# Chunked delta rule with raw keys and the inverse applied inside the scan, and another placing of the fill matmuls

## The reference

```python
g = jnp.cumsum(g.reshape(bsz, nh, n, CHUNK), axis=-1)
decay = jnp.exp(jnp.where(incl, g[..., :, None] - g[..., None, :], -jnp.inf))
kb = k * beta
a_mat = jnp.where(strict, jnp.einsum('bhncd,bhnsd->bhncs', kb, k) * decay, 0.0)
rhs = jnp.concatenate([v * beta, kb * jnp.exp(g)[..., None]], axis=-1)
sol = lax.linalg.triangular_solve(eye + a_mat, rhs, left_side=True, lower=True, unit_diagonal=True)
u_c, w_c = sol[..., :dv], sol[..., dv:]
...
def step(state, inp):
    v_new = u_i - jnp.einsum('bhcd,bhdv->bhcv', w_i, state)
    o_i = (jnp.einsum('bhcd,bhdv->bhcv', q_i, state)
           + jnp.einsum('bhcs,bhsv->bhcv', qk_i, v_new))
    state = state * jnp.exp(gl_i)[..., None, None] + jnp.einsum('bhcd,bhcv->bhdv', k_i, v_new)
    return state, o_i
...
o = _rms_norm(o_f + jnp.flip(o_b, 2), dn_gain)
```

## Time and profile before

| what | us |
|---|---|
| median of three runs | 3041.14 |
| lowest and highest | 3039.02, 3042.1 |
| span of the profiled execution | 3042.0 |
| own time of the profiled execution | not given apart from the span |
| PE busy in the span | 2950.7 |
| DVE, ACT, POOL busy | 2110.4, 1411.3, 488.3 |

### The profile page before, as it was taken

How to read it: one execution, slowest core, us unless ns; L and a number is a source line. 1 busy time by engine, 2 the same in 40 slices (tenths; PEclk the granted TensorE clock), 3 DMA queues, 4 the chain that set the end, 5 groups by cost and what they waited for, 6 DMA issues and landing times.

```text
span 3042.0 us, 51632 instructions
## 1 busy us (share of the span) xinstructions
PE 2950.7 (97%) x18980; PEld 2547.3 (84%) x18980; DVE 2110.4 (69%) x3097; ACT 1411.3 (46%) x2279; POOL 488.3 (16%) x392
## 2 busy tenths in 40 slices
PE   7999999999999999999999999999999999999998
PEld 4888888887789988777789988799988777799886
DVE  5566665446489954888789944799646986899635
ACT  3655565444356622334456622566423334566422
POOL 0213123157420011000200012100110000300012
PEclk9999999999999999999999999999999999999999
DMA  6121120213322322222323232232222222233322
GB/s 254 44 61 43 28 69 16 68 63 105 110 83 98 104 97 89 94 87 83 104 90 106 97 104 97 87 108 99 99 95 92 89 84 83 97 111 102 106 94 79
DMA packets 97248, 275.15 MB, mean 90 GB/s; under 512 B 35712, under 2 KB 36864, under 8 KB 95760
## 3 DMA queue, kind: packets, MB, share of 16 engines
q1 hardware_dynamic: 94016, 267.89, 26.5%
q10 hardware_dynamic: 2768, 4.25, 0.4%
q0 software_dynamic: 320, 1.05, 0.1%
HBM read 267.88 MB, written 5.28 MB: 90 GB/s over the span
## 4 chain that ended last, share of the span: by engine, by line
PE 87%; DVE 6%; ACT 4%; issue 2%; DMA 1%; SPq 0%; ACTq 0%; DVEq 0%
PE bank L149 16%; PE bank L151 16%; PE bank L150 16%; PE bank L2024 8%; PE bank L2025 8%; PE bank L2026 8%; PE bank L1598 1%; ACT weights_hi L137 1%; PE bank L1612 1%; PE bank L1664 1%; PE bank L2515 1%; DVE weights_lo L142 1%; PE bank L1667 1%; PE bank L1677 1%; DMA mod_weights<-w_mod 1%
## 5 line engine op out<-in xcount | busy, mean ns | idle before, releaser
L142 DVE TENSOR_TENSOR weights_lo<-weights_raw,weights_hi 128x1024 fp32r<-128x1024 f32 (+2 forms) x258 | 395.5, 1533 | 326.3 <-ACT weights_hi L137 323.0
L137 ACT ACTIVATE weights_hi<-weights_raw 128x1024 fp32r<-128x1024 f32 (+2 forms) x250 | 285.1, 1140 | 460.2 <-PE bank L151 447.8
L149 PE MATMUL bank<-x_hi,weights_hi 128*128 128x512 f32 x832 | 337.0, 405 | 5.1 <-DVE x_lo L1914 3.0
L151 PE MATMUL bank<-x_hi,weights_lo 128*128 128x512 f32 x832 | 326.4, 392 | 0.0
L150 PE MATMUL bank<-x_lo,weights_hi 128*128 128x512 f32 x832 | 325.3, 391 | 0.0
L2024 PE MATMUL bank<-sum_hi,block_hi 128*128 128x256 f32 x960 | 271.1, 282 | 4.6 <-ACT bank L2176 3.6
L150 PE MATMUL bank<-hidden_lo,weights_hi 128*128 128x512 f32 x704 | 273.9, 389 | 0.0
L149 PE MATMUL bank<-hidden_hi,weights_hi 128*128 128x512 f32 x704 | 273.9, 389 | 0.0
L151 PE MATMUL bank<-hidden_hi,weights_lo 128*128 128x512 f32 x704 | 273.9, 389 | 0.0
L2025 PE MATMUL bank<-sum_lo,block_hi 128*128 128x256 f32 x960 | 270.6, 282 | 0.0
L2026 PE MATMUL bank<-sum_hi,block_lo 128*128 128x256 f32 x960 | 269.4, 281 | 0.0
(11 more groups left out here) (451 smaller groups left out, 7466.4 us busy)
## 6 DMA issues: line engine op xcount, KB each, us to landing
raw_pair<-w_ff1in SPq DMA_DIRECT2D x42, 1024.0 KB, 4.9
raw_pair<-w_ff2in SPq DMA_DIRECT2D x42, 1024.0 KB, 4.9
weights_raw<-w_mix SPq DMA_DIRECT2D x72, 512.0 KB, 3.2
weights_raw<-w_ff1out SPq DMA_DIRECT2D x32, 704.0 KB, 4.0
weights_raw<-w_ff2out SPq DMA_DIRECT2D x32, 704.0 KB, 4.0
weights_raw<-w_tail SPq DMA_DIRECT2D x42, 512.0 KB, 3.3
mod_weights<-w_mod SPq DMA_DIRECT2D x6, 2048.0 KB, 16.4
weights_raw<-w_dn SPq DMA_DIRECT2D x24, 512.0 KB, 3.4
```

Source lines behind the costliest of these rows:

```text
L137: nc.scalar.activation(K.wh[:, slot, 0:cols], K.raw[:, slot, 0:cols], ACT.Copy).then_inc(S.wh_ready, 1)
L142: nc.vector.tensor_tensor(K.wl[:, slot, 0:cols], K.raw[:, slot, 0:cols], K.wh[:, slot, 0:cols].bitcast(F32), ALU.subtract).then_inc(S.raw_ ...
L149: nc.tensor.matmul(out, K.wh[:, slot, a:b], xh, start=start, stop=False)
L151: return nc.tensor.matmul(out, K.wl[:, slot, a:b], xh, start=False, stop=stop)
```

## The change

- The keys and queries stay raw (only silu), in `K.heads_kq`, double-buffered by group. The inverse squared key norm `K.n2` is multiplied in where systems and scores are formed, and into the decayed keys; the query norm is left to the head's final norm (`K.fq`). The transposes back and those of the decayed queries go.
- The solution is not formed. Each scan step multiplies the raw keys by the state (`against`), DVE forms the residual, PE multiplies it by the inverse (`renew`), ACT copies the new values out (`renewed`), and `grow` follows.
- Turning and systems are one loop. Tile t+1 is turned, its exponents written and its products made after the fill units of tile t. Keys and queries of all tiles go through bank 3, the exponents of all tiles through bank 4.
- Fill units: 4 more ahead of the first group, 2 per tile in the merged loop (1 in the last group), 5 in the end of the levels and up to 11 in the scan, from a budget of 12 (16 in the last two groups). The last group's scan takes the tail's slabs 8 and 9 (`AHEAD`).
- DVE's `conv` instructions are all done before the scan. The three calls of `act_head` and `act_center` inside the levels are at steps 2, 8 and 12 (two before, at 9 and 16).
- In the tail the sum of squares moves to DVE, the norm is applied by ACT on four tiles, and PE transposes the head's output instead of spreading the norm.

```diff
     def act_group(act, G):
+            if n > 0:
+                act.wait_ge(S.hss_ready, n)
+            nc.scalar.activation(K.junk[:, 0:w, :], pb[3][:, 0:128 * w].rearrange("p (c v) -> p c v", v=128), ACT.Square)\
                 .then_inc(S.hsq_ready, 1)
+            nc.scalar.activation(K.ks[:, t, 0:2, :], pb[3][:, 0:256].rearrange("p (c v) -> p c v", v=128), ACT.Copy)\
+                .then_inc(S.kt_ready, 1)
             act.wait_ge(S.tv_ready, n + 1)
+            nc.scalar.activation(K.vs[:, t, :, :], pb[7][:, 0:256].rearrange("p (j v) -> p j v", v=128), ACT.Copy)\
                 .then_inc(S.vs_ready, 1)
...
+        squares(0)
...
         for t in range(TILES):
-            if t < 4:
-                queries_back(t)
+            if t + 1 < TILES:
+                squares(t + 1)
             decays(t)
-            if t == 3 and not more:
-                act_gate(act, 1)
+            if t == 3 and more:
+                act_raw(act, G + 1, 1)
...
+        for n, (f, b, x) in enumerate(scan_steps()):
+            if n == 0:
+                continue
+            renewed(n, 0)
+            renewed(n, 1)
+            if x is not None:
+                state_out(x, (f, b))
+            if more and n in (2, 4):
+                act_head(act, G + 1, 3 + n // 2)
```

```diff
     def pe_group(pe, G, fills):
+        fill, later = fills[G], islice(fills[G + 1], 12 if G + 2 < GROUPS else 16)
         if G == 0:
             take(fill, 8)
             pe_sum_rows(pe)
+            take(fill, 4)
...
+        def turn_heads(t):
             n = TILES * G + t
+            if t > 0:
+                pe.wait_ge(S.kt_ready, n)
+            for c in range(4 if t < 4 else 2):
+                src = keys(G, c) if c < 2 else queries(G, c - 2)
+                last = nc.tensor.transpose(pb[3][:, 128 * c:128 * c + 128], src[:, lo:lo + 128], K.ident[:, :])
             last.then_inc(S.tk_ready, 1)
...
+        def rows(t):
             n = TILES * G + t
             if t > 0:
+                pe.wait_ge(S.dec_ready, n)
...
+        turn_heads(0)
+        rows(0)
+        products(0)
         for t in range(TILES):
-            if t < 4:
-                turn_queries(t)
-            rows(t)
-            products(t)
-            take(fill, 1)
+            take(fill, 2 if G < 3 else 1)
+            if t + 1 < TILES:
+                turn_heads(t + 1)
+                rows(t + 1)
+                products(t + 1)
         take(fill, 99)
...
+            if i > STEPS_INNER:
+                take(later, 1)
         correction(STEPS_LEVEL - 1)
...
         for n, (f, b, x) in enumerate(scan_steps()):
+            if n == 0:
                 continue
+            tiles = (f, b)
+            for d, t in enumerate(tiles):
+                against(n, d, t)
+            if x is not None:
+                answer(n, x, tiles)
+            take(later, 1)
+            if n == 1:
+                pe.wait_ge(S.e_ready, STEPS_LEVEL * (G + 1) + CREDIT)
+            for d, t in enumerate(tiles):
+                renew(n, d, t)
+            take(later, 2)
             if n < 5:
+                for d, t in enumerate(tiles):
+                    grow(n, d, t)
+            if x is not None:
+                if x == 0:
+                    pe.wait_ge(S.qkd_ready, 4 * G + 4)
+                inner(n, x, tiles)
+        pe.wait_ge(S.oa_ready, 4 * G + 4)
         pe.wait_ge(S.ot_ready, 8 * G + 8)
```

```diff
     def dve_group(dve, G):
         if more:
-            split_lo(dve, s + 1, 1, 1024)
-            take(conv, 8)
+            take(conv, 4)
...
             ins.then_inc(S.e_ready, 1)
-            take(conv, 1 if i < STEPS_INNER + 2 else 2)
+            take(conv, 1 if i < STEPS_FIRST else 2)
...
         state_start()
     def pe_tail(pe):
             elif kind in "up":
-                pe_slab(pe, a, b, slot, False)
+                if i not in AHEAD:
+                    pe_slab(pe, a, b, slot, False)
...
             if i in NORMED:
                 n = NORMED[i]
-                pe.wait_ge(S.nrstd_ready, n + 3)
+                pe.wait_ge(S.hsc_ready, n + 1)
                 if n > 0:
-                    pe.wait_ge(S.on_ready, n)
+                    pe.wait_ge(S.zs_used, gates_until(n - 1))
                 for t in range(4):
+                    last = nc.tensor.transpose(pb[5][:, 128 * t:128 * t + 128], K.ot[:, n, t, :], K.ident[:, :])
                 last.then_inc(S.head_wide, 1)
```

More of the change, by code:

```diff
@@ L2 @@
 from contextlib import ExitStack
-from itertools import chain
+from itertools import chain, islice
 import numpy as np
@@ L511, in make_first_memory @@
     K.dd = put("inverse_turned", [128, 3, 4, 128])
+    K.otmp = [put(f"state_out{i}", [128, 4, 128], F32, w0 + 6144 + 2048 * i) for i in range(2)]
+    K.rr = put("residual", [128, 4, 128], F32, w0 + 10240)
     K.pp = put("product", [128, 2, 256])
@@ L1148, in dve_group, with norms @@
         s = DN_SLAB + 6 * G + 8
-        def squares(t):
+        def norms(t):
             n = TILES * G + t
@@ L1234, in dve_group @@
             split_lo(dve, s + 4, 0, 1024)
+            take(conv, 6)
         else:
@@ L1670, in grow @@
-        def grow(n, tiles):
+                pe.wait_ge(S.vm_ready, G + 1)
+                pe.wait_ge(S.e_ready, STEPS_LEVEL * G + STEPS_INNER + d + 1 + CREDIT)
+            for j in range(2):
+                c = 2 * d + j
+                last = nc.tensor.matmul(pb[scan_bank(n, d)][:, part(j)], K.e[:, c, t, :], K.rr[:, c, :] if n else K.vs[:, t, j, :],
+                                        start=True, stop=True)
+            last.then_inc(S.uw_made, 1)
+        def grow(n, d, t):
+            pe.wait_ge(S.vn_ready, 12 * G + 2 * n + d + 1)
+            for j in range(2):
+                c = 2 * d + j
+                last = nc.tensor.matmul(pb[scan_bank(n, d)][:, part(j)], K.ks[:, t, c, :], K.vn[:, c, :], start=True, stop=True)
+            last.then_inc(S.su_ready, 1)
@@ new lines, in against, with answer @@
+        def against(n, d, t):
+            pe.wait_ge(S.st_ready, 10 * G + 2 * n + d - 1)
+            for j in range(2):
+                c = 2 * d + j
+                last = nc.tensor.matmul(pb[scan_bank(n, d)][:, part(j)], keys(G, j)[:, 128 * t:128 * t + 128], K.st[1 - n % 2][:, c, :],
+                                        start=True, stop=True)
+            last.then_inc(S.sk_ready, 1)
+        def answer(n, x, tiles):
+            if x > 0:
+                pe.wait_ge(S.oa_ready, 4 * G + x)
@@ L1712, in pe_group @@
-            against(n, (f, b))
-            if x == 3:
-                take(later, 2)
-            if x > 0:
-                pe.wait_ge(S.ot_ready, 8 * G + 2 * x)
-            for c, t in enumerate((f, f, b, b)):
-                nc.tensor.matmul(pb[7][:, part(c)], K.st[1 - n % 2][:, c, :], K.qd[:, t, c, :], start=(c == 0), stop=False)
-            if n < 5:
-                grow(n, (f, b))
-            else:
-                for d in range(2):
-                    pe.wait_ge(S.vn_ready, 2 * (5 * G + n) + d - 1)
@@ L1724, in pe_group @@
-            for c, t in enumerate((f, f, b, b)):
-                last = nc.tensor.matmul(pb[7][:, part(c)], K.vn[:, c, :], K.qkd[:, t, c, :], start=False, stop=(c == 3))
-            last.then_inc(S.so_ready, 1)
-        take(later, 2)
+            tiles = (f, b)
+            for d, t in enumerate(tiles):
+                against(n, d, t)
+            if x is not None:
+                answer(n, x, tiles)
+            take(later, 1)
+            if n == 1:
+                pe.wait_ge(S.e_ready, STEPS_LEVEL * (G + 1) + CREDIT)
```

460 lines of the change are left out of this document (205 added, 255 removed).

## The result

The changed kernel takes 3099.41 us (median of 4 runs, 3097.3 to 3102.53), the kernel before in the same session 3041.55 (4 runs, 3039.02 to 3042.1). The ratio is 1.0193, with a 95% interval of 1.0179 to 1.0208. It is slower by 58 us where 36.5 were forecast; 3099 is inside the range of 3044 to 3108. That it is slower is far outside the noise; whether it is slower by a full 2% is not settled by the interval.

What follows compares the result with a forecast made beforehand. PE, busy 97% of the span, was taken as the bound. Added 104.9 us (waits and half clock) less 68.4 removed gave net 36.5 on 3042.0, less 0.9: 3078 us, range 3044 to 3108.

Steps and rivals of the forecast that it cites:

- sign that would have told of slack: Cover's end: PE waiting there for the inverse's DMA would mean that the lost time was slack and the forecast wrong.
- Work removed: PE, groups and tail: fewer solution matmuls and transposes, 39.5 us in all, plus 8 counted in the tail: 47.5.
- Waits before the decay rows: Merged loop: PE waits ACT's whole turn in each tile, 12.2 us a group, 49 in four; bounds 35 to 60.
- half clock after them: After the 20 tile waits: three quarters followed by a half-clock stretch, 20 x 1.25 = 25 us, between 0 and 34.
- Scan start: Step 1 waits for DVE's state copy behind two convs: 3.0 in three groups, 1.1 last, plus half clock; 14.6 us.
- Scan waits: Inside the scan: 0.5 in step 5, 0.25 in step 2, 0.85 at the group's end; 5.6 us in all.
- Interruptions of the levels: Levels: a third `act_head` and `act_center`, about 1.0 us a group in three groups; 3 added.
- Tail start: Head 0's transposes wait 6.8 us in place of 0.84, with 1.7 of half clock; 7.7 added.
- The rest of the tail: Tail heads: four transposes replace one-column and diagonal matmuls, 1.1 us a head, 9 in all, 8 counted as saved.
- rule of the Trainium skill that the prediction names: Tile waits: warns only of longer idle gaps, so waits of 2.3 us would leave the clock alone and cost it nothing.
- 15.8 removed: Idle part of the 20.9 us of gaps removed around groups, turning, systems and scans; two thirds of 23.5 idle.
- rival of the falling clock: Tile waits: every wait leaves two half-clock stretches, 20 us more, 3098 us; chance 0.12.

Runs made afterwards that it cites:

- experiment 1: Changed kernel with ACT issuing the exponentials of tile t ahead of the square and copies of tile t+1: 3030.05 us, ratio 0.9959.
- eighth kernel: Changed kernel with exponentials first, no convolution just ahead of the scan, one tail slab left in the tail, heads one and two later: 3004.00 us, ratio 0.9872.
- second experiment: Changed kernel with matmuls that nobody reads run by PE between the next tile's transposes and its decay rows: 3066.34 us, ratio 1.0082.
- third experiment: Changed kernel with DVE's convolution instructions of the last three level steps moved into the first scan steps: 3090.67 us, ratio 1.0157.
- fifth experiment: Changed kernel with ACT's work for the next group's heads one and two level steps later (2, 9, 14): 3088.39 us, ratio 1.0156.
- fourth experiment: Changed kernel with only slab 8 computed in the last scan, slab 9 left in the tail: 3092.43 us, ratio 1.0162.
- experiments 1 to 11: All follow-up runs but the last, each the changed kernel with one or more edits: between 2999.75 and 3103.32 us.
- twelfth: Changed kernel with all seven edits: the four combined ones, two more in split and fill order, and POOL held back in the tail: 2997.84 us, ratio 0.9855.
- tenth experiment: The four-edit kernel (3004) with the last group's first fill split ahead of the norms and first-tile fill behind the second tile's transposes: 2999.75 us, ratio 0.9861.
- three experiments that gained nothing: Changed kernel with, separately, tail order edits (3100.92 us), one ACT scaling in place of four (3103.32), POOL's fifth-grid sums held back (3099.85).
- sixth kernel: Changed kernel with each tile's fill units moved behind the next tile's transposes, ahead of its decay rows: 3045.76 us, ratio 1.0010.
- eleventh experiment: Changed kernel with POOL's sums over the tail's fifth grid held until DVE made the fourth pooled input's low part: 3099.85 us, ratio 1.0192.

## Why the prediction was near, and where it failed

Direction and mechanism were right: the waits in the tiles and the clock behind them decided, and without them the changed kernel is faster than the one before (experiment 1). The sign that would have told of slack, PE waiting for the inverse's DMA at the cover's end, is not in the changed kernel's trace. The size was 21 us short.

- **Work removed, 47.5.** As work it holds: 50.6 in the eighth kernel, less up to 3.4 for the clock, is 47 to 51. That all of it would shorten the kernel does not hold in the tail, as said below.
- **Waits before the decay rows, 49.** Measured 43.4. The first tile was 3.26 to 3.53 (forecast 3.56), the others 1.62 to 2.05 in place of 2.05 to 2.28. At full clock they were 2.05 and 1.83: the forecast left out that PE makes the two value transposes while ACT already works on the square, 0.2 us of overlap. At half clock these transposes take longer and more of ACT's turn is hidden, down to 1.62.
- **The half clock after them, 25 (0 to 34).** Mis-sized, at the top of its own bounds: 34 by the second experiment, 32 by the first. It left 78 us at half clock around 20 waits (119.4 less 41.0), 23 stretches where I had counted 15. By the rule of the Trainium skill that the prediction names ("TensorE: Matmul & The Clock Gate", "Why this matters for your kernels") it should have come at most behind the four longest waits, those of the first tiles, 3.26 to 3.53; the trace has it around waits of 1.62 to 2.05 too, and the second experiment puts the price of all of it at 34 us. (The prediction counted nothing by that rule, though its own first-tile wait of 3.56 is of the length of these four.)
- **Scan start, 14.6.** Right: 10.7 idle for 10.1, and with the clock about 5, by the third experiment.
- **Scan waits, 5.6.** Right: 0.56 four times and 0.89 three times, and small ones.
- **Interruptions of the levels, 3.** This step failed. I priced ACT's instructions and not what they wait for: DVE's convolution was not done when ACT came to it. Idle time there is 9.5 us (0.51, 1.86 and 0.6 to 0.9 in each of three groups) where it was 2.1, so 7.4 more for the 3 of the forecast; with the half clock behind two of the waits of 1.86 the term is about 11. The fifth experiment got 11 back, of which its trace accounts for some 9 here (5.9 idle and the clock of two stretches).
- **Tail start, 7.7.** The wait was 8.16 and not 6.8, with 10.2 us at half clock around it; 9 by the fourth experiment.
- **The rest of the tail, -8 for work and nothing else.** This step failed too: PE's work is not what sets the time there. Its waits grew from 7.0 us (2.25, 1.47, 2.82 and 0.43) to 12.7 (0.64, 0.67, 4.65, 3.48, 1.36, 1.08 and 0.84); each head's deviation now goes through DVE and ACT and not through PE. From PE's start behind the wait for the pooled low part to the second `pool_mixed` eviction the kernel before takes 80.5 us and the changed one 80.1, though PE is busy for 2.5 us less in it. In the traces of experiments 1 to 11 it takes 79.7 to 80.2, whatever happens to the single waits, and 82.5 in the twelfth's.
- **The last group's first fill slab**, which isn't in the forecast: 2.85 of idle time, at weights that DVE splits behind its norms; in the tenth experiment, with the split first, it is gone.

In sum, over the stretch of the ledger: idle time was forecast at +58 (49 + 10.1 + 5.6 + 6.0 + 3 added, 15.8 removed) and was +67 (-5.6 tiles, +4.4 levels, +1.3 and +5.8 tail, +2.9 last group). The clock was forecast at +26 (25 + 4.5 + 1.7 added, 5.1 removed) and was 36 to 39, which is the work removed, 47 to 51, less the 11.6 by which busy time fell. That the tile waits were 5.6 us too high hid a part of the miss. The rival of the falling clock gave 3098, which is nearly the time measured, but its reason, two stretches behind every wait, is not what happened: there were 23 and not 40, and more than half of the miss lies in waits that have nothing to do with the tiles.

Which chain bounds the middle of the tail can be read, though no experiment shortened it. The chain of work that ended last, in the changed kernel (start, us, what):

```profile
759.97 5.46 DVE pool_mixed L1366 x4
...
771.82 6.78 DVE mixed_lo L1334 x5
...
794.68 9.10 DMA weights_raw<-w_tail
```

and in the kernel before:

```profile
703.39 4.92 DVE pool_mixed L1331 x4
...
714.01 7.56 DVE mixed_lo L1304 x5
...
740.05 8.13 DMA weights_raw<-w_tail
```

It runs through DVE's products and low parts behind the first `pool_mixed` eviction and then through a transfer of weights, in both kernels alike, so work taken from PE beside it becomes waiting. The order at step 17 and the contention at the fourth pooled input lie ahead of these steps, and ACT's scaling is 1.3 us a head between them, which fits the three experiments that gained nothing. What shorter steps of DVE would give is not shown.

## What to carry to other kernels

When a helper engine's queue holds both an answer that PE waits for and a request that needs PE's next output, put the answer first; or put independent PE work between the request and the wait. Both recover the loss (71 and 56 us, experiments 1 and 6), and the idle time is only about half of it while short waits cost clock. When a step is moved, price what the moved instruction waits for at its new place, not only its length; and take a wait in front of a longer chain as slack until an experiment has removed it. Work taken from the busiest engine counts only where the chain that ended last runs through that engine: here 2.5 us of it in the tail bought 0.4.

## What the hardware showed that was not expected

- **Filling a wait with useless matmuls gained 34 us** at unchanged waiting time (1.0193 to 1.0082). In the eighth kernel no wait up to 1.50 us was followed by a stretch at half clock, those of 4.65, 3.13 and 2.61 were, and one of 2.84 was not; in the changed kernel waits of 1.62 to 2.05 were, though not all. The length of a wait alone doesn't decide: the wait of 2.05 at the third tile of group three has no such stretch behind it in the changed kernel's trace, and in the third experiment's, where it is 2.04, it has two.
- **DVE's instructions get longer beside POOL's.** A `weights_lo` of 128 x 1024 takes 1.23 us alone and 2.17 beside POOL's sums. The Trainium skill ("Trainium Architecture — The Big Picture", "What this means for kernel authors") says that the two share a port pair as an exclusive lock. The eleventh experiment agrees that they hold each other up there, as holding POOL back took 2.2 us out of three DVE instructions; whether by a lock or by sharing, no run here tells.
- **One execution of the sixth kernel took 5974.97 us** where its others took 3043 to 3049. There is no trace of it and it is unexplained. The ratio leaves it out; the median of 3045.76 would be 3045.57 without it.
